# Samples' state products with C stationary in column groups, states loaded two slots ahead, a chunk's sums moved back within its slot: a state-space layer of a hybrid decoder

## The reference, cut to what matters

```python
adt = ...(dt * a)                     # 32 heads, 4 groups of B and C, 128 states
a_cum = jnp.cumsum(adt, axis=-1)
cb = jnp.einsum('bcign,bcjgn->bcgij', c, b)
w = cb[:, :, :, None] * jnp.exp(segsum(adt))
y_diag = jnp.einsum('bcgrij,bcjgrp->bcigrp', w, xdt)
...
y_off = jnp.einsum('bcign,bcgrpn,bcgri->bcigrp', c, new_states[:, :-1], jnp.exp(a_cum))
y = (y_diag + y_off).reshape(bt, L, H, P)
```

## Time and profile before

| what | us |
|---|---|
| median of 3 runs (lowest, highest) | 2106.91 (2106.85, 2110.78) |
| the profiled execution's own time | 2107.75 |
| its span, first to last instruction | 2106.1 |
| granted TensorE clock, mean | 0.953 of full |
| TensorE busy | 1934.6 (92% of the span) |
| VectorE, ScalarE, GpSimd busy | 1186.1, 960.5, 478.6 |

### The profile page before, as it was taken

One profiled execution on the slowest core, in us unless ns is written; L12 is line 12 of the kernel. 1 busy time (PEld: TensorE's weight loads), 2 busy tenths in 40 slices (PEclk: granted clock), 3 DMA queues, 4 the chain that ended last, 5 costly groups with the idle time before them and its releaser, 6 DMA issues. The chain is left out here.

```text
span 2106.1 us, 37643 instructions
## 1 busy us (share of the span) xinstructions
PE 1934.6 (92%) x14726; PEld 1830.9 (87%) x14726; DVE 1186.1 (56%) x2046; ACT 960.5 (46%) x1566; POOL 478.6 (23%) x480
## 2 busy tenths in 40 slices
PE   6899979999998678999997887999998999799999
PEld 4899969999997457999996666999988999699998
DVE  4677764555443235554445775555466777555543
ACT  3666663444342124443343554444347666434432
POOL 3222212333100002442102321333112222023420
PEclk9999989999998688999999998999999999899999
DMA  6367755555552094655656742665563667456554
GB/s 181 98 203 235 235 173 161 160 163 147 172 170 79 17 275 122 169 161 144 176 192 206 288 170 76 176 169 152 164 191 113 221 218 222 135 154 166 161 150 133
DMA packets 502033, 352.63 MB, mean 167 GB/s; under 512 B 14154, under 2 KB 487100, under 8 KB 501084
## 3 DMA queue, kind: packets, MB, share of 16 engines
q1 hardware_dynamic: 495156, 306.03, 49.9%
q0 software_dynamic: 6272, 43.92, 5.5%
q10 hardware_dynamic: 430, 0.29, 0.1%
HBM read 326.58 MB, written 50.63 MB: 179 GB/s over the span
## 5 line engine op out<-in xcount | busy, mean ns | idle before, releaser
L268 PE MATMUL ps<-xh,whi 128*128 128x288 f32 x2368 | 657.8, 304 | 10.0 <-PEq L176 9.9
L268 PE MATMUL ps<-xl,whi 128*128 128x288 f32 x2368 | 647.1, 300 | 0.0
L240 DVE TENSOR_TENSOR wlo<-raw,whi 128x2048 fp32r<-128x2048 f32 (+3 forms) x241 | 501.8, 2083 | 245.2 <-ACT whi L229 245.0
L229 ACT ACTIVATE whi<-raw 128x2048 fp32r<-128x2048 f32 (+3 forms) x241 | 419.1, 1740 | 263.5 <-PE ps L276 231.4
L268 PEld LDWEIGHTS ps<-xh,whi 128*128 128x128 f32 x2368 | 454.7, 192 | 12.2 <-issue 10.5
L268 PEld LDWEIGHTS ps<-xl,whi 128*128 128x128 f32 x2368 | 455.4, 192 | 0.8
L276 PE MATMUL ps<-xh,wlo 128*128 128x288 f32 x2368 | 354.6, 300 | 0.0
L276 PEld LDWEIGHTS ps<-xh,wlo 128*128 128x128 f32 x2368 | 328.8, 190 | 1.1
L520 POOL TENSOR_TENSOR gh<-sg,ut 128x288 f32<-128x288 f32 x88 | 216.3, 2458 | 353.0 <-ACT sg L461 353.0
L268 PE MATMUL ps<-hh,whi 128*128 128x288 f32 x704 | 189.7, 296 | 0.0
L268 PE MATMUL ps<-hl,whi 128*128 128x288 f32 x704 | 189.6, 297 | 0.0
(11 more groups left out here) (319 smaller groups left out, 2702.4 us busy)
## 6 DMA issues: line engine op xcount, KB each, us to landing
raw<-in_ffn_w_in SPq DMA_DIRECT2D x176, 512.0 KB, 5.0
raw<-in_ssm_w_in SPq DMA_DIRECT2D x80, 512.0 KB, 4.8
raw<-in_ffn_w_out SPq DMA_DIRECT2D x64, 384.0 KB, 4.0
raw<-in_ffn_w_out SPq DMA_DIRECT2D x64, 320.0 KB, 3.2
H<-in_state_ssm SPq DMA_DIRECT2D x32, 512.0 KB, 7.6
out_ssm_sample<-H SPq DMA_DIRECT2D x32, 512.0 KB, 6.5
raw<-in_ssm_w_out SPq DMA_DIRECT2D x32, 512.0 KB, 5.0
Kp_L<-in_cache_diff_k SPq DMA_DIRECT2D x64, 256.0 KB, 4.5
```

The lines of the kernel that those rows point to most:

```text
L229: act.activation(wts["hi"][:, s, 0:width], raw[:, s, 0:width], ACT.Copy).then_inc(hi_ready.sem, 1)
L240: dve.tensor_tensor(wts["lo"][:, s, 0:width], raw[:, s, 0:width], wts["hi"][:, s, 0:width].bitcast(F32), ALU.subtract).then_inc(lo_ready.s ...
L268: pe.matmul(out, W[0][:, kk, j, :], x_[:, k, :], stop=False, start=(part == 0 and kk == 0 and x_ is seg.hi), skip_group_check=True)
```

## The change

Three things, all in the state-space layers:

1. y_state has C as stationary operand. Cz holds, for each group and sample, 32 columns of which only the sample's own 4 are not zero (filled once by POOL, `spread_c`), and the state HT moves with 128 columns. The samples are dealt to three column groups of the array (output rows 32 to 63, 64 to 95, 96 to 127 of bank 5, columns 256 to 383), and accumulate there. Two new copies of ACT per chunk, `move_ys`, bring the three partial results into rows 32 to 127 of XU's plane 5, where zeros lay; the matching rows of cb are 1 and those of the mask constant pick each token's own row, so that y_inside's third product scales and adds them. DVE's `take` works on 128 instead of 160 columns.
2. SP loads the states of chunk k+2 instead of k+1, at the end of its turn, after waiting for the store of the chunk k-2 that it has just issued.
3. On PE turn_x, spread(2k) and spread_chunk(k) stand ahead, y_state(k-1) and sums_of_chunk(k-1) behind them, all before the second 16 block matmuls. On ACT move_s0, move_fs and the new move_ys stand behind decay(2k) instead of behind `ahead`. turn_state(k, 0) waits for move_fs and now for move_ys too, since it overwrites bank 5.

Some small tiles move into free parts of G to make room for Cz.

```diff
-                    if 4 <= k + 1 < CI:
-                        sp.wait_ge(h_out[(k + 1) % 4].sem, h_out[(k + 1) % 4].at((k + 1) // 4))
-                        load_state(k + 1)
                     if k >= 3 and k % 2:
                         store_final(k // 2 - 1)
+                    if 4 <= k + 2 < CI:
+                        sp.wait_ge(h_out[(k + 2) % 4].sem, h_out[(k + 2) % 4].at((k + 2) // 4))
+                        load_state(k + 2)
...
                         pe.wait_ge(fs_moved.sem, fs_moved.at(c))
+                        pe.wait_ge(ys_moved.sem, ys_moved.at(2 * c))
...
-                def y_state(c, half):
+                def y_state(c):
                     pe.wait_ge(h_moved.sem, h_moved.at(2 * c + 2))
...
-                    for b in range(4 * half, 4 * half + 4):
-                        at = TOK + P + b * T
-                        mm = pe.matmul(ps[:, 7, at:at + T], HT[:, b, :],
-                                       BC[:, GROUPS + c // 4, SEQ + b * T:SEQ + (b + 1) * T],
-                                       start=True, stop=True, skip_group_check=True)
+                    for b in range(NB):
+                        o = 32 * (1 + b % 3)
+                        mm = pe.matmul(ps[o:o + NS, 5, 2 * P:3 * P], Cz[:, c // 4, b, :], HT[:, b, :], start=(b < 3),
+                                       stop=(b + 3 >= NB), tile_position=(0, o), skip_group_check=True)
                     mm.then_inc(ys_mm.sem, ys_mm.inc())
...
                     more(L)
-                    sums_of_chunk(k - 1)
-                    more(L)
                     turn_x(k)
-                    more(L)
-                    y_state(k - 1, 0)
-                    more(L)
-                    y_state(k - 1, 1)
                     more(L)
                     spread(2 * k)
                     spread_chunk(k)
                     more(L)
+                    y_state(k - 1)
+                    sums_of_chunk(k - 1)
+                    more(L, 2)
                     outer_half(k - 1, 0)
...
+                def move_ys(c):
+                    act.wait_ge(ys_mm.sem, ys_mm.at(c + 1))
...
+                    for lo, hi in ((NS, 64), (64, P)):
+                        act.activation(XU[lo:hi, c % 2, 5, :], ps[lo:hi, 5, 2 * P:3 * P], ACT.Copy).then_inc(
+                            ys_moved.sem, ys_moved.inc())
...
-                    else:
-                        move_s0(k - 1)
-                        move_fs(k - 1)
...
                     decay_chunk(k)
                     decay(2 * k)
+                    if k >= 1:
+                        move_s0(k - 1)
+                        move_fs(k - 1)
+                        move_ys(k - 1)
                     move_state(k, 0)
```

More of the change, by code:

```diff
@@ L765, in ssd @@
             BC, xr = sb("BC", [P, 2 * GROUPS, TOK]), sb("xr", [P, 4, TOK])
-            Bt, Bs = sb("Bt", [P, 2, GROUPS * N_STATE]), sb("Bs", [NS, GROUPS * N_STATE])
+            Bt, Cz = sb("Bt", [P, 2, GROUPS * N_STATE]), sb("Cz", [P, GROUPS, NB, NS])
             BtS, Bm = sb("BtS", [3 * NS, GROUPS * N_STATE], F32R), sb("Bm", [P, NB, N_STATE], F32R)
@@ L769, in ssd @@
             XU, dmul = sb("XU", [P, 2, 7, P]), sb("dmul", [P, 7, HEADS])
-            dtk, adk, nack = (sb(n, [P, 3, HEADS]) for n in ("dtk", "adk", "nack"))
-            arg, dec, ea, Dd = sb("arg", [P, 4, HEADS]), sb("dec", [P, 4, HEADS]), sb("ea", [HEADS, 1 + HEADS]), sb("Dd", [HEADS, 2, CI])
+            dtk, adk, arg, dec = (G[:, 8 + n, 96:96 + k * HEADS].rearrange("p (k h) -> p k h", h=HEADS)
+                                  for n, k in enumerate((3, 3, 4, 4)))
+            nack = sb("nack", [P, 3, HEADS])
+            ea, Dd = sb("ea", [HEADS, 1 + HEADS]), sb("Dd", [HEADS, 2, CI])
             acHL, cb = sb("acHL", [P, TOK], F32R), sb("cb", [P, GROUPS, TOK])
@@ L776, in ssd @@
             E, EA = sb("E", [P, 4, TOK]), sb("EA", [P, 2, P + NS])
-            yo, yt, sq = sb("yo", [P, P + NS]), sb("yt", [P, 3, TOK]), sb("sq", [P, 4, TOK])
+            yo, yt, sq = sb("yo", [P, P]), sb("yt", [P, 3, TOK]), sb("sq", [P, 4, TOK])
+            Bs = sq.rearrange("p c n -> p (c n)")[0:NS, 0:GROUPS * N_STATE]
             rs, dsk = sb("rs", [P, 2, TOK]), sb("dsk", [P, CI])
@@ L782, in ssd @@
             strow = H[0:3 * NB, 0:3, :, :].rearrange("p r b n -> p (r b n)")
-            padded = S("rows_padded")
+            padded, ys_moved = S("buffers_filled"), S("probs_scaled")
             tri, tris, same = (cst[:, c:c + P] for c in (C_TRI, C_TRIS, C_SAME))
@@ L1009, in spread @@
                         pe.wait_ge(dec_args.sem, dec_args.at(2))
-                        pe.wait_ge(padded.sem, padded.at(4))
+                        pe.wait_ge(padded.sem, padded.at(5))
                     if h % 2 == 0 and c >= 7:
@@ L1072, in y_inside @@
                     pe.wait_ge(w_ready.sem, w_ready.at(2 * c + 2))
+                    pe.wait_ge(ys_moved.sem, ys_moved.at(2 * c + 2))
                     r = c % 2
@@ L1166, in _ @@
                         turn_tail(1)
+                y_state(CI - 1)
                 sums_of_chunk(CI - 1)
-                y_state(CI - 1, 0)
-                y_state(CI - 1, 1)
                 outer_half(CI - 1, 0)
@@ L1184, in _, with spread_c @@
                 pool.memset(sp_[:, 0, 64:96], 0.0).then_inc(zeroed.sem, zeroed.inc())
-                pool.memset(cb[:, :, SEQ:TOK], 0.0).then_inc(zeroed.sem, zeroed.inc())
+                pool.memset(cb[:, :, SEQ:TOK], 1.0).then_inc(zeroed.sem, zeroed.inc())
                 pool.memset(XU[:, :, 5, :], 0.0).then_inc(padded.sem, padded.inc())
+                pool.memset(Cz[:, :, :, :], 0.0).then_inc(padded.sem, padded.inc())
+                def spread_c():
+                    pool.wait_ge(padded.sem, padded.at(5))
+                    pool.wait_ge(conv_ready.sem, conv_ready.at(EARLY + 1))
+                    own = Cz.rearrange("p g b n -> p g (b n)")
+                    for g in range(GROUPS):
+                        ins = pool.tensor_copy(
+                            bass.AP(own.tensor, own[:, g, 0:1].offset, [own.ap[0], [NS + T, NB], [1, T]]),
+                            BC[:, GROUPS + g, SEQ:TOK].rearrange("p (b t) -> p b t", t=T))
+                    ins.then_inc(padded.sem, padded.inc())
                 def conv_ends(n):
@@ L1222, in _ @@
                         conv_ends(n)
+                    if k == 0:
+                        spread_c()
                     weigh(2 * k)
@@ L1324, in move_state @@
                     act.wait_ge(h_turned.sem, h_turned.at(2 * c + half + 1))
-                    act.wait_ge(ys_mm.sem, ys_mm.at(2 * c))
+                    act.wait_ge(ys_mm.sem, ys_mm.at(c))
                     act.activation(HT[:, 4 * half:4 * half + 4, :], ps[:, 5, :], ACT.Copy).then_inc(
@@ L1337, in move_fs @@
                     act.activation(Fs[:, c % 4, :], ps[:, 5, P:2 * P], ACT.Copy).then_inc(fs_moved.sem, fs_moved.inc())
+                def move_ys(c):
+                    act.wait_ge(ys_mm.sem, ys_mm.at(c + 1))
+                    if c == 0:
+                        act.wait_ge(padded.sem, padded.at(5))
+                    if c >= 2:
+                        act.wait_ge(y_mm.sem, y_mm.at(2 * c - 2))
+                    for lo, hi in ((NS, 64), (64, P)):
+                        act.activation(XU[lo:hi, c % 2, 5, :], ps[lo:hi, 5, 2 * P:3 * P], ACT.Copy).then_inc(
+                            ys_moved.sem, ys_moved.inc())
                 def pick_rows(c):
@@ L1435, in _ @@
                 move_fs(CI - 1)
+                move_ys(CI - 1)
                 for c in range(4):
@@ L1580, in spread_x @@
                     if c == 0:
-                        dve.wait_ge(padded.sem, padded.at(4))
+                        dve.wait_ge(padded.sem, padded.at(5))
                     dve.wait_ge(x_turned.sem, x_turned.at(c + 1))
@@ L1628, in take @@
                     dve.wait_ge(off_added.sem, off_added.at(c))
-                    dve.tensor_tensor(yo[:, :], ps[:, 7, TOK:TOK + P + NS], EA[:, c % 2, :], ALU.mult).then_inc(
+                    dve.tensor_tensor(yo[:, :], ps[:, 7, TOK:TOK + P], EA[:, c % 2, 0:P], ALU.mult).then_inc(
                         off_scaled.sem, off_scaled.inc())
@@ L1632, in take @@
                     dve.wait_ge(y_taken.sem, y_taken.at(c + 1))
-                    dve.tensor_tensor(yt[:, r, P:TOK], yt[:, r, P:TOK], yo[:, :], ALU.add).then_inc(
+                    dve.tensor_tensor(yt[:, r, P:2 * P], yt[:, r, P:2 * P], yo[:, :], ALU.add).then_inc(
                         off_added.sem, off_added.inc())
@@ L2905, in shape_constants @@
     c[:NS, C_TRIS:C_TRIS + NS] = same & (s[:, None] <= s[None])
+    c[NS:, C_TRIS:C_TRIS + NS] = i[NS:, None] % NS == i[None, :NS]
     c[:NS, C_SAME:C_SAME + NS] = same
```

4 lines of the change are left out of this document (1 added, 3 removed).

## The result

The changed kernel takes 2133.82 us (median of four runs, 2130.05 to 2135.79) against 2108.85 for the kernel before (four runs): ratio 1.0109, 95% interval 1.0085 to 1.0134. It is 1.1% slower. The prediction had 2103.5 with a range of 2090 to 2113.

A forecast was written before the change was run, and what follows sets the result against it. It took a loop through DVE's and ACT's lists over a pair of slots, not PE, as the limit after the change. Pairs -11.4, loop ends +2, old falls -6, new falls +12: -3.4 from 2106.9 gives 2103.5 us, range 2090 to 2113.

The forecast's parts named there:

- PE's wait at `turn_state` in z slots: PE, arriving at 18.0, waits 2.4 us for ACT's copies out of bank 5, done so that turn_state starts at 20.46.
- the load: States' load two slots ahead on SP: counted as 0, since it lands before the chunk wants it.
- slot 15 and the tail: End of the loop: work now behind the root's wait at the lower clock, +1.0 per layer, +2 in all.
- the four old falls: Clock falls behind the old y_state in z slots, taken to vanish with it: 4 x 1.5 = -6 us.
- In the x slot no table load stands in ACT's way ... no wait: At turn_state in x slots: ACT's copies done at 6.7, PE arrives at 6.75, so PE doesn't wait.
- six pairs (slots 3 to 14) in two layers: The saving of 0.95 us per pair applied to all pairs alike: 12 x 0.95 = -11.4.
- the pair: An x slot plus a z slot, set by DVE's and ACT's lists: 24.84 us against 25.79, -0.95.
- the slow rival: Copies' wait lowers the clock nearly each time, 14 falls: 2112.5, or 2116 with ACT's list 0.3 longer per pair; chance 0.17.
- Mis-sized: y_state: Its 16 instructions on PE take 0.6 us instead of 1.71, upper bound 0.66 if groups overlap; 1.1 less per chunk.
- slots 1 and 2 at 0, within 1 per layer: Start of the loop: slot 1 waits some 2.8 us, slot 2 gets that back, so no net cost.
- 14 new waits: Waits at turn_state, 12 of 2.4 us and two of some 2.8, bring 8 clock falls at 1.5: +12.
- Column groups don't overlap: Rival: y_state stays at about 1.7, the pair at 24.8, the wait shrinks to 1.3: about 2092; chance 0.13.

The follow-up runs named there:

- e5: The kernel before with only the states' load moved two slots ahead: 2108.74 us, ratio 0.9989.
- e9: The changed kernel with the states loaded one slot ahead, as before the change: 2133.07 us, ratio 1.0100.
- e4: The kernel before with the change's order on PE and place of ACT's two copies; old y_state, load one slot ahead: 2126.39 us, ratio 1.0075.
- e1: The changed kernel with the spreads of slots 7, 11 and 15 back behind the second run of block matmuls: 2126.42 us, ratio 1.0063.
- e8: The changed kernel with e1's spreads and ACT's bank 5 copies right behind split_u, ahead of the root: 2071.12 us, ratio 0.9821.
- e2: The changed kernel with ACT's copies out of bank 5 ahead of decay_chunk and the exponentials: 2091.44 us, ratio 0.9881.
- e10: The changed kernel with all of y_state in one column group and one ACT copy instead of two: 2123.56 us, ratio 1.0057.
- e6: The kernel before with the column-group y_state, then the sums, ahead of turn_x; copies early on ACT, load one slot ahead: 2116.38 us, ratio 1.0026.
- e11: e8 with the states loaded one slot ahead instead of two: 2080.82 us, ratio 0.9852.

## Why the prediction was wrong, by its own steps

- **What held.** PE's wait at `turn_state` in z slots, ended by ACT's XU: 2.23 for 2.4. Start of the x slot to silu 12.29 for 12.23 (126.56 to 138.85); `turn_state` to L1086 4.38; ACT's list up to the copies 7.36 for 7.41; no wait that the profile lists in plain x slots (one of 0.15 is hidden there, see y_state below); no fall behind y_state; the load 0 (e5, e9); slot 15 and the tail +2.0 in sum over both layers, for +2. That the old form of y_state made the four old falls is not shown: e4 keeps it and has none in its z slots.
- **The step that failed**: "In the x slot no table load stands in ACT's way ... no wait", multiplied by "six pairs (slots 3 to 14) in two layers". It was read from slot 9, and two of the six pairs start with a slot that has the root. The prediction put the spreads' wait for the root only into slot 15. In slots 7 and 11 it is 2.59, and it lowers the clock each time: +3.5 in each of four slots instead of about -1.1. Together with the z slots behind them, (17.72 + 13.32) - 27.70 = +3.3 per pair where the prediction had -0.95: +17 for the four. e1 and e8 show the cause (with the spreads behind the second run, slots 7 and 11 have no root wait), and e4 shows it without the column groups. Of the 30.8 between the forecast's -3.4 and the trace's +27.4 these pairs are 17, slots 0 and 1 are 9, the plain pairs 4, the stretches outside the loops 4, and the falls behind `turn_state` -3 (6 instead of 8).
- **Mis-sized: the pair.** 13.78 + 11.55 = 25.33 instead of 24.84. The four copies with their signal take 1.30 on ACT, not 0.82: the two new ones, of 32 and 64 rows, start 0.33 behind Fs and the last ends 0.57 later, and they were priced by the step of 0.155 between the two old ones. The other price at hand, a copy at its own length, was used only in the slow rival, as 0.3.
- **Mis-sized: y_state.** 0.78, not 0.6; 0.66 was called the upper bound. The plain x slot lost 0.67, not 1.11: 0.18 of the missing 0.44 is y_state's length. Another 0.18 goes at `turn_state`: in slot 3 L1039 starts 0.38 behind L1059, in e2, whose copies stand earlier, 0.23, and there the plain x slot takes 11.37. So the x slot's "6.7" and "6.75: no wait" had no room for the longer copies. The last 0.09 goes ahead of y_state: the first L1068 starts 0.16 behind the last spread, where L1055 started 0.07 behind it before.
- **Wrong: slots 1 and 2 at 0, within 1 per layer.** From `products_cb` to the first L1086 it is 19.9 and 21.6 for 16.25. Across the 12 profiles all 16 such stretches with the change's order take 18.4 to 21.6, and five of the eight with the old order 15.8 to 16.3; the other three, with a low clock there, 19.0 to 20.8. The means are 19.9 and 17.5, so some 2.4 us a layer go with the order; all 16 have a stretch at the low clock and only three of the eight others do. Why the clock is low there with the change's order was not found out.
- **The falls.** 14 new waits were to bring 8. In slots 2 to 14 there are 6 behind the waits at `turn_state` and 4 behind the root's. That part of the estimate was near; what it lacked were the waits themselves.
- **+3.7 outside the loops** lies between the layers and at the ends. It is no larger than what the profiles differ by (the stretch between the layers is 1297 to 1309 in these profiles), and no run speaks for a cause.
- **The rivals.** The slower one (2112.5 to 2116) took the right sign, from clock falls; its ceiling was too low since it had the same pairs under it. "Column groups don't overlap" was wrong in its premise but right about the mechanism (e10): PE's gain in y_state was worth nothing where ACT sets the wait. Its numbers were as far off as the forecast's, since it had the same pairs: 1.3 of waiting and 2092, where e10 has 0.3 and 2123.6.

## What to carry to other kernels

When an edit pulls an instruction forward in its engine's stream, list every semaphore it waits on and the iterations in which that wait is real; read the iterations with extra work (here the root in slots 7 and 11) from their own rows, not from a plain one. When a result moves later on the engine that drains it, the producer's bank is held that much longer: place the drain where its input is ready, ahead of work that nobody waits for so soon. Two waits in one iteration hide each other, so the repair of one alone can measure small (7 of 63 us for the root's here); and a faster producer pays only after the drain has been moved, while it exposes loads (e6) that were hidden before.

## What the runs showed of the hardware

A copy of 128 x 48 on GpSimd takes 0.24 in slot 1 of the first layer of the changed kernel and 2.29 in the second. DVE's timeline and ACT's stand behind POOL's:

```profile
103.34 0.24 POOL L1204 COPY ec<-stT 128x48 f32<-128x48 f32 x1
...
1629.34 2.29 POOL L1204 COPY ec<-stT 128x48 f32<-128x48 f32 x1
```

```profile
1629.14 2.40 DVE L240 TENSOR_TENSOR wlo<-raw,whi 128x2048 fp32r<-128x2048 f32 x1
```

```profile
1631.71 1.19 ACT L1251 ACTIVATE ec<-ec,vec 128x312 f32<-128x312 f32 x2 [4.09 <-issue]
```

```profile
1637.25 1.08 PE L1039 MATMUL ps<-cst,H 128*128 128x128 f32 x4 [4.95 <-ACT XU L1358]
```

The copy ends at 1631.63, 0.09 behind DVE's subtraction, which started 0.20 before it. ACT's taps need the copied columns and start 0.08 later, and the wait at `turn_state` in that slot is 4.95 where it is 1.60 in the first layer. Of these 3.35 the copy's delay is 2.05 (ACT idles 4.09 ahead of the taps, 2.04 in the first layer); the rest is that PE comes 1.3 earlier in ACT's list. The Trainium skill (SBUF — State Buffer, Summary: rules for kernel authors) says that where DVE has two SBUF inputs while the GpSimd instruction reads SBUF, the second one to issue fully blocks until the first finishes; this trace agrees. In the kernel before a copy of the tail took 2.55 in slot 1 (nobody waits for that one), and there the rows differ from that rule: it started at 102.30, 0.19 ahead of DVE's subtraction (102.49, 2.27 long), and still ended 0.09 behind it. So a start of 0.2 ahead was not enough. In the first layer the copy starts 1.1 ahead of DVE's instruction (104.44), in the second 0.2 behind it: 1.3 in phase decide over 2 us.

Whether the clock falls is not settled by the wait's length alone, nor by the slot: the same 2.23 at `turn_state`, with the same work on both sides, was followed by a fall in slots 6, 10 and 14 and not in slot 4; in the second layer of e9 slot 4 has the fall (15.29 at 0.89) and slot 6 has not (13.81 at 1.00). The longest wait in slots 2 to 14 of any profile, 3.52 for H in slot 14 of e11's second layer, had none. PE's row and the slot's window:

```profile
1770.77 0.66 PE L1039 MATMUL ps<-cst,H 128*128 128x128 f32 x4 [3.52 <-DMA H<-in_state_ssm]
```

```profile
1760.07:1775.20 15.13, 11.61 (x104) 10.65 (x103) 8.06 (x19) 9.78 (x23) 1.69 (x3) 1.00 0.81 248
```
